# A two-layer conv and attention model on one core: the first two units of the first stage run side by side, on smaller transfers

## The reference, cut to what matters

```python
def rmsnorm(x, g):
    y = x * rsqrt(mean(x * x, axis=-1) + EPS)
    return y * g

def short_conv_mixer(h, w_in, conv_w, w_out):      # h = rmsnorm(x, mix_norm[0]), [256, 1024]
    bg, cg, v = split(h @ w_in, 3)                 # w_in is [1024, 3072]
    return (bg * causal_dwconv(cg * v, conv_w)) @ w_out

for layer in range(2):
    if layer == 0:
        x = x + short_conv_mixer(...)
    else:
        kv = nsa_shared_kv(rmsnorm(x, kv_norm), ...)
        x = x + nsa_mixer(rmsnorm(x, mix_norm[1]), ..., kv, rel_bias)
    x = x + conv_ffn(rmsnorm(x, ffn_norm[layer]), ...)
return rmsnorm(x, final_norm)
```

## Time and profile before

| | us |
|---|---|
| median of three runs | 679.98 |
| span of the profiled execution | 678.8 |
| runs above that span | 1.18 |
| TensorE busy | 661.2 (97%), 5178 matmuls |
| weight loads busy | 630.0 (93%) |
| VectorE busy | 491.6 (72%) |
| ScalarE busy | 370.1 (55%) |
| GpSimd busy | 75.6 (11%) |
| HBM read | 106.43 MB, 158 GB/s over the span |

### The profile page before, as it was taken

The page is one execution under the profiler, slowest core; times in us unless marked ns, Lnnn a source line. Parts: engine busy times, 40 slices in busy tenths (PEclk is TensorE's granted clock), DMA queues, the critical chain, the costliest instruction groups (busy, mean ns, idle before and its releaser), DMA issues.

```text
span 678.8 us, 14195 instructions
## 1 busy us (share of the span) xinstructions
PE 661.2 (97%) x5178; PEld 630.0 (93%) x5178; DVE 491.6 (72%) x961; ACT 370.1 (55%) x695; POOL 75.6 (11%) x100
## 2 busy tenths in 40 slices
PE   7999999999999999999999999999999999999994
PEld 7999999999999999999798776688999999999994
DVE  4787566888877777765986766616788887777755
ACT  6654345666655555565664657615665655555532
POOL 1100012000000000031231334411100000000012
PEclk9999999999999999999998999999999999999998
DMA  8687353266555557713483110003255665555301
GB/s 318 238 302 246 108 187 111 104 233 206 202 188 183 185 185 267 252 39 105 160 316 115 64 32 0 1 1 125 94 188 186 223 224 200 179 182 180 140 32 62
DMA packets 30351, 107.98 MB, mean 159 GB/s; under 512 B 3387, under 2 KB 3659, under 8 KB 30316
## 3 DMA queue, kind: packets, MB, share of 16 engines
q1 hardware_dynamic: 29756, 105.39, 44.2%
q0 software_dynamic: 560, 2.12, 0.9%
HBM read 106.43 MB, written 1.07 MB: 158 GB/s over the span
## 4 chain that ended last, share of the span: by engine, by line
PE 89%; DVE 6%; ACT 2%; DMA 1%; issue 1%; SPq 0%; DVEq 0%; ACTq 0%
PE bank L957 26%; PE bank L959 25%; PE bank L958 25%; DVE w_lo L684 2%; PE bank L1241 1%; PE bank L1245 1%; PE bank L1216 1%; DMA staged<-in_a_up 1%; ACT w_hi L495 1%; PE bank L1043 1%; PE bank L1242 1%; PE bank L1189 1%; PE bank L1187 1%; PE bank L1186 1%; DVE rstd L722 1%
## 5 line engine op out<-in xcount | busy, mean ns | idle before, releaser
L957 PE MATMUL bank<-gx,w_hi 128*128 128x256 f32 x1024 | 291.4, 285 | 5.0 <-DVE w_lo L684 3.8
L959 PE MATMUL bank<-gx,w_lo 128*128 128x256 f32 x1024 | 289.7, 283 | 0.0
L958 PE MATMUL bank<-gx,w_hi 128*128 128x256 f32 x1024 | 289.7, 283 | 0.0
L684 DVE TENSOR_TENSOR w_lo<-staged,w_hi 128x1024 fp32r<-128x1024 f32 x191 | 233.8, 1234 | 41.9 <-ACT w_hi L495 41.7
L495 ACT ACTIVATE w_hi<-staged 128x1024 fp32r<-128x1024 f32 x197 | 199.3, 1043 | 31.6 <-PE bank L959 22.0
L957 PEld LDWEIGHTS bank<-gx,w_hi 128*128 128x128 f32 x1024 | 196.5, 192 | 8.2 <-DVE w_lo L684 4.6
L958 PEld LDWEIGHTS bank<-gx,w_hi 128*128 128x128 f32 x1024 | 196.5, 192 | 0.1
L959 PEld LDWEIGHTS bank<-gx,w_lo 128*128 128x128 f32 x1024 | 196.5, 192 | 0.0
L958 PE MATMUL bank<-y,w_hi 128*128 128x256 f32 x416 | 117.7, 283 | 0.0
L957 PE MATMUL bank<-y,w_hi 128*128 128x256 f32 x416 | 117.7, 283 | 0.0
L959 PE MATMUL bank<-y,w_lo 128*128 128x256 f32 x416 | 117.7, 283 | 0.0
(11 more groups left out here) (143 smaller groups left out, 672.0 us busy)
## 6 DMA issues: line engine op xcount, KB each, us to landing
staged<-in_f_up SPq DMA_DIRECT2D x88, 512.0 KB, 5.2
staged<-in_f_down SPq DMA_DIRECT2D x44, 512.0 KB, 3.3
staged<-in_a_up SPq DMA_DIRECT2D x24, 512.0 KB, 6.5
staged<-in_b_up SPq DMA_DIRECT2D x24, 512.0 KB, 4.5
staged<-in_a_down SPq DMA_DIRECT2D x8, 512.0 KB, 3.4
staged<-in_b_down SPq DMA_DIRECT2D x8, 512.0 KB, 4.2
bias<-bias_rows POOLq DMA_DIRECT2D x1, 2048.0 KB, 10.3
x<-in_xT SPq DMA_DIRECT2D x4, 256.0 KB, 5.3
```

The lines of the kernel that those rows point to most:

```text
L684: nc.vector.tensor_tensor(w_lo[:, q["slot"], 0:n], staged[:, s, 0:n], w_hi[:, q["slot"], 0:n].bitcast(F32), ALU.subtract).then_inc(lo, 1)
L957: nc.tensor.matmul(out_ap, whi, xhi, start=start, stop=False, skip_group_check=True)
L958: nc.tensor.matmul(out_ap, whi, xlo, start=False, stop=False, skip_group_check=True)
L959: return nc.tensor.matmul(out_ap, wlo, xhi, start=False, stop=stop, skip_group_check=True)
```

## The change: what it does

Units 0 and 1 of stage a are multiplied side by side: TensorE uses `together` with six products, row block by row block, the norm ahead of the last row block, the bias rows' matmul after it. x comes in 8 transfers of one row block (1 KB per partition), the weights of both units in 8 transfers of one row block of all six pieces (six times 512 B per partition, the first one in two halves), from an array laid out for it by the host, all in the order of the row blocks. ScalarE and VectorE cut the six pieces by row blocks too (384 columns twice for the first, 768 for the next six), and by pieces of 128 columns for the last. The gains and taps of stage a come in a first transfer of 72 columns, the other parameters after all of x and these weights. The norm's sum goes to bank 5, since bank 3 is now in use. Unit 2 and all behind it stay as they are, in the order of the queues too.

```diff
--- before.py
+++ after.py
@@ -98,7 +98,7 @@
                 slot = UP_SLOTS + (u % 3 if st != "a" else {AU - 2: 2, AU - 1: 0}.get(u, u % 2))
-            turns[slot] = turns.get(slot, 0) + 1
+            turns[slot] = turns.get(slot, -1 if kind == "up" else 0) + 1
             table[key] = dict(n=n, slot=slot, turn=turns[slot], prev=used.get(slot))
@@ -123,7 +123,7 @@
-def build(nc, xT, par, hot, rel, a_up, a_down, f_up, f_down, b_up, b_down, scratch, out):
+def build(nc, xT, par, hot, rel, a_first, a_up, a_down, f_up, f_down, b_up, b_down, scratch, out):
     piece = plan_pieces()
@@ -192,8 +192,10 @@
         landed = [sem(f"landed{s}") for s in range(UP_SLOTS + 1)]
-        x_landed = [sem(f"x_landed{b}") for b in range(4)]
-        par_landed, hot_landed, bias_landed = sem("par_landed"), sem("hot_landed"), sem("bias_landed")
+        first_landed = [sem(f"first_landed{k}") for k in range(KT)]
+        second_landed = sem("second_landed")
+        first_hi, first_lo = sem("first_hi"), sem("first_lo")
+        gains_landed, par_landed, hot_landed, bias_landed = sem("gains_landed"), sem("par_landed"), sem("hot_landed"), sem("bias_landed")
         hi_up, lo_up, used_up = sem("hi_up"), sem("lo_up"), sem("used_up")
@@ -281,7 +283,7 @@
-        NORM_BANK = {"a": 3, "f0": 3, "b": 3, "f1": 7, "end": 7}
+        NORM_BANK = {"a": 5, "f0": 3, "b": 3, "f1": 7, "end": 7}
         ACC_BEFORE = {"f0": ACC["a"], "b": ACC["f0"], "f1": ACC["b"], "end": ACC["f1"]}
@@ -322,20 +324,22 @@
-            def x_tiles(b):
-                sp.dma_start(x[:, 2 * b:2 * b + 2, :], xT[:, 2 * b:2 * b + 2, :]).then_inc(x_landed[b], 16)
-
-            x_tiles(0)
-            sp.dma_start(params[:], par).then_inc(par_landed, 16)
-            x_tiles(1)
-            load("a", "up", 0, 0)
-            x_tiles(2)
-            x_tiles(3)
-            load("a", "up", 0, 1)
-            load("a", "up", 0, 2)
+            def first(kt, units=slice(0, 2)):
+                six = slice(3 * units.start, 3 * units.stop)
+                return sp.dma_start(staged[:, six, kt * P:kt * P + P], a_first[kt, :, six, :])
+
+            early = PAR["f_taps"]
+            sp.dma_start(params[:, 0:early], par[:, 0:early]).then_inc(gains_landed, 16)
+            for kt in range(KT):
+                sp.dma_start(x[:, kt, :], xT[:, kt, :]).then_inc(first_landed[kt], 16)
+                if kt == 0:
+                    first(kt, slice(0, 1)).then_inc(first_landed[kt], 16)
+                    first(kt, slice(1, 2)).then_inc(second_landed, 16)
+                else:
+                    first(kt).then_inc(first_landed[kt], 16)
+            sp.dma_start(params[:, early:NPAR], par[:, early:NPAR]).then_inc(par_landed, 16)
             sp.dma_start(hot_sb, hot).then_inc(hot_landed, 16)
             sp.dma_start(table_sb[0:BUCKETS, :], rel).then_inc(hot_landed, 16)
-            ups("a", 1)
             for k in (2, 3):
@@ -494,6 +498,20 @@
+            def first_lead(kt):
+
+                act.wait_ge(first_landed[kt], 32)
+                nc.scalar.activation(gx_hi[:, kt, :], x[:, kt, :], ACT.Copy, scale=gain(GAIN_OF["a"], kt)).then_inc(gx_hi_done, 1)
+                cols = slice(kt * P, kt * P + P)
+                if kt == KT - 1:
+                    for n in range(6):
+                        nc.scalar.activation(w_hi[:, n, cols], staged[:, n, cols], ACT.Copy).then_inc(hi_up, 1)
+                    return
+                for six in ((slice(0, 3), slice(3, 6)) if kt == 0 else (slice(0, 6),)):
+                    if kt == 0 and six.start:
+                        act.wait_ge(second_landed, 16)
+                    nc.scalar.activation(w_hi[:, six, cols], staged[:, six, cols], ACT.Copy).then_inc(first_hi, 1)
+
             def norm(st, between=(), meanwhile=()):
@@ -505,21 +523,17 @@
                 if st == "a":
-                    act.wait_ge(par_landed, 16)
-                    for b in range(4):
-                        act.wait_ge(x_landed[b], 16)
-                        leads(b)
-                        if b == 1:
-                            lead("a", "up", 0, 0)
-                    for q in between:
-                        lead(*q)
+                    act.wait_ge(gains_landed, 16)
                 if st == "end":
...
                         act.wait_ge(x_new, 4 * (k - 1) + b + 1)
-                    if st not in ("a", "end"):
+                    if st == "a":
+                        first_lead(2 * b)
+                        first_lead(2 * b + 1)
+                    elif st != "end":
                         leads(b)
@@ -597,9 +611,10 @@
-            norm("a", between=UPS("a", 0)[1:], meanwhile=UPS("a", 1))
+            norm("a")
             stage("a", UPS("f0", 0) + UPS("f0", 1))
             norm("f0", meanwhile=SOON("f0"))
+            act.wait_ge(par_landed, 16)
             stage("f0", B_PIECES(0, 4))
@@ -684,6 +699,22 @@
+            def first_rest(kt):
+
+                cols = slice(kt * P, kt * P + P)
+                if kt == KT - 1:
+                    for n in range(6):
+                        dve.wait_ge(hi_up, n + 1)
+                        nc.vector.tensor_tensor(w_lo[:, n, cols], staged[:, n, cols], w_hi[:, n, cols].bitcast(F32),
+                                                ALU.subtract).then_inc(lo_up, 1)
+                    return
+                for six in ((slice(0, 3), slice(3, 6)) if kt == 0 else (slice(0, 6),)):
+                    dve.wait_ge(first_hi, kt + (2 if six.stop == 6 else 1))
+                    if kt == 0 and six.start:
+                        dve.wait_ge(second_landed, 16)
+                    nc.vector.tensor_tensor(w_lo[:, six, cols], staged[:, six, cols], w_hi[:, six, cols].bitcast(F32),
+                                            ALU.subtract).then_inc(first_lo, 1)
+
             def norm(st, between=(), meanwhile=()):
@@ -701,17 +732,18 @@
                     residual(1)
+                else:
+                    dve.wait_ge(gains_landed, 16)
                 for b in range(4):
...
                             if st == "a":
-                                dve.wait_ge(par_landed, 16)
-                                dve.wait_ge(x_landed[b], 16)
+                                dve.wait_ge(first_landed[kt], 32)
                             nc.vector.scalar_tensor_tensor(gx_lo[:, kt, :], x[:, kt, :], gain(GAIN_OF[st], kt),
                                                            gx_hi[:, kt, :].bitcast(F32), ALU.mult, ALU.subtract).then_inc(gx_lo_done, 1)
-                    if st == "a" and b == 1:
-                        rest("a", "up", 0, 0)
+                            if st == "a":
+                                first_rest(kt)
                     if st != "a" and b < 2:
@@ -795,12 +827,13 @@
             nc.vector.memset(table_sb[BUCKETS:BUCKETS + 1, :], NEG).then_inc(table_done, 1)
-            norm("a", between=UPS("a", 0)[1:], meanwhile=UPS("a", 1))
+            norm("a")
             dve.wait_ge(rows_done, 1)
...
             norm("f0", meanwhile=SOON("f0"))
+            dve.wait_ge(par_landed, 16)
             stage("f0", B_PIECES(0, 4))
@@ -958,14 +991,11 @@
-            def product(q, dst, xh, xl, first, move=0, fresh=None, hi_sem=None):
+            def product(q, dst, xh, xl, first, move=0):
...
                 for kt in range(KT):
-                    if fresh is not None:
-
-                        pe.wait_ge(fresh, hi_sem + kt + 1)
                     mm = three(dst, w_hi[:, s, kt * P:kt * P + P], w_lo[:, s, kt * P:kt * P + P],
@@ -978,7 +1008,6 @@
             def up(st, k, i=0):
-                fresh = (gx_lo_done, 8 * NORM[st]) if k == 0 else (None, None)
                 ring = 2 if st == "a" else 3
@@ -986,19 +1015,25 @@
                     dst, first = up_place(st, k, c)
-                    product(piece_of(st, "up", k, c), dst, gx_hi, gx_lo, first, move, *fresh)
+                    product(piece_of(st, "up", k, c), dst, gx_hi, gx_lo, first, move)
...
-                for q, dst, first in todo:
-                    pe.wait_ge(lo_up, q["n"] + 1)
+                if st != "a":
+                    for q, dst, first in todo:
+                        pe.wait_ge(lo_up, q["n"] + 1)
                 for kt in range(KT):
...
                         norm(st)
-                    for q, dst, first in todo:
+                    for n, (q, dst, first) in enumerate(todo):
                         s = q["slot"]
+                        if st == "a":
+                            if kt == KT - 1:
+                                pe.wait_ge(lo_up, q["n"] + 1)
+                            elif n in ((0, 3) if kt == 0 else (0,)):
+                                pe.wait_ge(first_lo, kt + (1 if n == 0 and kt == 0 else 2))
                         mm = three(dst, w_hi[:, s, kt * P:kt * P + P], w_lo[:, s, kt * P:kt * P + P], gx_hi[:, kt, :],
@@ -1051,15 +1086,13 @@
                 if st == "a":
-                    up(st, 0)
-                    norm(st)
```

(4 more changed lines are left out.)

## The result

The changed kernel takes 682.27 us (median of nine runs, 681.62 to 683.74), the kernel before 679.98: a ratio of 1.0039 with a 95% interval from 1.0029 to 1.0048. It is 2.3 us slower, clear of noise and inside the stated range. The forecast was 680.9 with "same" (within 1.4 us) as its likeliest outcome; the outcome was "slower". Repeated in another series beside the kernel before it had a ratio of 1.0059 (1.0043 to 1.0075).

What follows compares the result with a forecast made beforehand. TensorE bounds the kernel (89% of the span); early start, waits for data and the uncovered norm chain put unit 2 at 31.6 to 32.0 against 30.93. Taking +0.9 us on the median 679.98 gave 680.9, range 679.1 to 684.0.

Steps and rivals of the forecast that it cites:

- The chain of 5.9 us: Between the sum of squares and unit 2: norm chain loses unit 1's cover, takes 5.9 us, TensorE stands for 3.0.
- 31 to 32: Sign of being right: S, the time in us at which TensorE starts unit 2, lies between these.
- Row block 1: Second row block of paired units: operands ready at 11.0, TensorE wants them at 9.6, so 1.4 us idle.
- not before 7.3: TensorE's first product cannot start earlier, as the untouched warm-up is ahead in its queue.
- Row blocks 2 to 7: Block 2 ready at 12.5 to 13.6 against 13.2; from block 3 nothing waits; last squares done near 23.4.
- The price of small rows: Weight transfers in 512 B rows: 0.032 us per packet, so a row block costs 1.95 us per engine.
- the line: Packet price drawn through 4 KB (0.165 us) and 1.5 KB (0.070 us) packets: 0.038 us per KB.
- the first rival, dear small rows: 512 B packets cost over 0.036 us, so data sets the last block; 685.1 us at 0.045; chance 0.37.
- SP's queue: SP issues a transfer every 0.47 us; the last weights go out 18th, at 8.8, at no cost.
- N: End of the norm's sum of squares on TensorE, forecast at 25.7 to 26.1 us.
- the +0.3 to +1.1 of the prediction: Change in us of unit 2's start against 30.93 in the kernel before; +0.9 was taken.
- the forecast's own 681.3: Upper end of the forecast's own range, 680.2 to 681.3 us; the forecast had chance 0.45.

Runs made afterwards that it cites:

- norm chain alone: The kernel before, with only the norm's and bias rows' matmuls moved behind unit 1's products, the norm's sum in bank 5: 687.42 us, ratio 1.0125.
- the changed kernel again: The changed kernel as it is, timed again beside runs of the kernel before: 683.06 us, ratio 1.0059.
- filled behind the norm: The changed kernel with 13 unread matmuls of ones behind the bias rows' matmul, where TensorE stands before unit 2: 681.91 us, ratio 1.0024.
- norm early: The changed kernel with the norm's matmuls ahead of row block 6 instead of 7: 682.89 us, ratio 1.0059.

## Why the prediction was right, and where its centre was off

**The chain of 5.9 us: right.** From the end of the sum of squares (27.62) to unit 2 (33.55) it took 5.93, with 3.05 us of idle TensorE against 3.0. The run with the norm chain alone shows it without the rest of the change. It is what eats the 3.3 us of earlier start. Unit 2's start itself, 33.55, lies outside the 31 to 32 that was given as a sign of being right; the clock, below, is why.

**Row block 1: right in time, short in the wait.** It was ready at 11.05 (11.0 predicted). But the first product started at 6.69, not 7.4, so the wait was 2.1 us and not 1.4. The bound "not before 7.3" was wrong: the warm-up ended at 6.89 here and near 7.9 in other executions, so its end is no fixed point.

**Row blocks 2 to 7: right.** Nothing waited for data behind row block 1, in the second profile of the changed kernel either, where TensorE was at full rate there. The last squares were done at 21.4, earlier than the 23.4 of the sum.

**The price of small rows: close, a little high.** Packets between 6 and 9 us of the changed kernel:

```profile
DMA packets 1590, 0.89 MB, mean 298 GB/s; under 512 B 47, under 2 KB 1590, under 8 KB 1590
...
q1 hardware_dynamic: 1590, 0.89, 98.0%
```

1590 less 47 small ones in 98.0% of 48 us are 0.0305 us each; six of seven are 512 B and one is 1 KB, for which the line gave 0.035. The 0.036 from which the first rival, dear small rows, would have set the end was not reached. The rule of the Trainium skill ("DMA: Bandwidth & Descriptors", Specifications) that 512 B moves at line rate does not hold here: 298 GB/s with all engines busy, against the 404 GB/s of 4 KB packets in the earlier trace rows.

**SP's queue: wrong, without effect.** The last weights were to be issued at 8.8. They went out at 13.33:

```profile
6.49 1.86 SPq L334 DMA_DIRECT2D x<-in_xT  x1
...
13.33 0.60 SPq L329 DMA_DIRECT2D staged<-in_a_first  x1
...
20.99 1.30 SPq L317 DMA_DIRECT2D staged<-in_a_up  x3
```

One issue of x took 1.86 us, three others about 1.0, where the sum had 0.47 for each; what held SP back is not shown. The data still came early enough for TensorE, so nothing came of it. Unit 2's loads went out at 20.99 (22 predicted) and ScalarE, which started on them at 28.06, waited for none.

**The clock: missing.** This is the step that failed. The sum priced an idle stretch at its length: 1.4 us for row block 1 and 3.0 us before unit 2. In the profile each is followed by 16 matmuls at half rate, 1.5 us more. N, predicted at 25.7 to 26.1, was 27.62: that less 1.5 is 26.1. In three profiles with 512 B rows, no filler ahead of row block 1 and no half rate behind it, unit 2 started at 31.21 (the changed kernel again), 31.76 (filled behind the norm) and 32.00 (norm early, which gained nothing): 0.3 to 1.1 us over 30.93, the +0.3 to +1.1 of the prediction. The middle of these and one half-rate stretch make 0.8 + 1.5 = 2.3 us, and with the 0.4 us at the end of the kernel 2.7; measured were 2.3 in the first series and 3.5 between the medians of the second. How the executions of the medians lost their clock was not seen one by one, so the sum is an estimate. The Trainium skill, "TensorE: Matmul & The Clock Gate", section "HAM oscillation — how this bites in real kernels", describes a kernel whose matmuls wait some 3 to 5 us for data between bursts and start each next burst at the lower rate. The trace agrees in direction, with shorter waits (2.1 and 3.05 us of idle, then 0.21 us per matmul): the page would have named the term, and its price comes from the rows here.

So the verdict "slower" came neither from dear rows, the rival that was given 0.37 for it, nor from late data, but from the forecast's own mechanism with a term left out. That 682.27 still lies in the stated range is luck in part: above the forecast's own 681.3 the range had been drawn for dear rows.

## What to carry to other kernels

Before units of work are paired to start earlier, look at what the second one was covering: here it hid a serial chain of 5.7 to 5.9 us, and uncovering that cost more than the 3.3 us of early start gave. When one chain is shortened, read the queue of the waiting engine for the next one; moving the norm alone gave nothing, moving it with the bias rows gave 1.7 us. Price an idle stretch of TensorE of 2 to 3 us at its length plus 1.5 us that may follow at the lower clock. And where single executions differ by losses of 1.5 us that no edit made, compare many of them, with their clocks, before a trace of one is called a gain.

## What the runs showed of the hardware that was not expected

The clock does not follow the length of a gap alone. In the kernel before, 2.7 us of idle ahead of 10.00 were followed by full rate; with the same program up to there, the run of the norm chain alone had 2.43 us and then the half rate (0.58 for the first matmul, where it is 0.36 to 0.39 at full rate):

```profile
10.44 0.58 PE L957 MATMUL bank<-gx,w_hi 128*128 128x256 f32 x1 [2.43 <-DVE w_lo L684]
```

VectorE's gx_lo took 1.41 and 1.52 us in two of its eight times (0.48 in the others), both overlapping GpSimd's additions of squares, which also grew from 1.37 to 1.54 and 1.67. GpSimd, then VectorE:

```profile
14.10 1.54 POOL L402 TENSOR_TENSOR sumsq<-sumsq,work 128x512 f32<-128x512 f32 x1 [12.18 <-ACT work L547]
17.54 1.67 POOL L402 TENSOR_TENSOR sumsq<-sumsq,work 128x512 f32<-128x512 f32 x1 [1.90 <-ACT work L547]
...
14.51 1.41 DVE L743 SCALAR_TENSOR_TENSOR gx<-x,params,gx 128x256 fp32r<-128x256 f32 x1
...
17.98 1.52 DVE L743 SCALAR_TENSOR_TENSOR gx<-x,params,gx 128x256 fp32r<-128x256 f32 x1
```

Both times VectorE's operation ended 0.3 us behind GpSimd's (15.92 and 15.64, 19.50 and 19.21), as if it had waited for it; no run tests that. In the kernel before, GpSimd's additions overlapped only the last 0.1 us of an operation of VectorE. It was off the path here.
